# SBUF slots moved to multiples of 512 B, and a router with stationary weights in four column groups, in a two-block fp32 network on one core

## What is computed

```
def ec_moe(x, w_router, w_gate, w_up, w_down):
    B, N, _ = x.shape
    cap = CAPACITY_FACTOR * N // N_EXPERTS
    aff = jax.nn.softmax(jnp.einsum('bnd,de->bne', x, w_router).astype(jnp.float32), axis=-1)
    gates, idx = lax.top_k(jnp.swapaxes(aff, 1, 2), cap)
    bidx = jnp.arange(B)[:, None, None]
    xin = x[bidx, idx]
    h = jax.nn.silu(jnp.einsum('becd,edf->becf', xin, w_gate)) * jnp.einsum('becd,edf->becf', xin, w_up)
    out = jnp.einsum('becf,efd->becd', h, w_down) * gates[..., None].astype(x.dtype)
    return jnp.zeros_like(x).at[bidx, idx].add(out.astype(x.dtype))
```

## Time and profile before

| | us |
|---|---|
| median of 3 runs | 1737.58 (1735.65 to 1738.44) |
| the profiled execution's own time | 1737.63 |
| its span, first to last instruction | 1735.3 |
| TensorE busy | 1392.9 (80%) |
| VectorE busy | 593.1 (34%) |
| ScalarE busy | 431.6 (25%) |
| router of stage 0, and of stage 1 | from about 137, and from about 742 |
| units of stage 0 and of stage 1 reach their end | about 585, and about 1186 |

### The profile page before, as it was taken

One profiled execution on the slowest core, in us unless ns is written; L12 is line 12 of the kernel. 1 busy time (PEld: TensorE's weight loads), 2 busy tenths in 40 slices (PEclk: granted clock), 3 DMA queues, 4 the chain that ended last, 5 costly groups with the idle time before them and its releaser, 6 DMA issues.

```text
span 1735.3 us, 21553 instructions
## 1 busy us (share of the span) xinstructions
PE 1392.9 (80%) x9012; PEld 912.1 (53%) x9012; DVE 593.1 (34%) x993; ACT 431.6 (25%) x702; POOL 42.1 (2%) x53
## 2 busy tenths in 40 slices
PE   8999565574655999995765656559999999999997
PEld 8786121121211675751211212117999989889996
DVE  5663000010000366530000000004555566865556
ACT  4552000000000333420000000002444355653343
POOL 2000000000010012000000000000000000000000
PEclk9999888787888999998877878879999999999999
DMA  9858999999999943589999999999465764245650
GB/s 339 240 239 352 423 422 423 423 424 423 422 404 425 384 176 121 243 361 423 423 422 423 423 424 422 422 424 338 150 201 174 248 200 139 74 139 177 193 193 24
DMA packets 151333, 533.69 MB, mean 308 GB/s; under 512 B 10220, under 2 KB 73980, under 8 KB 105052
## 3 DMA queue, kind: packets, MB, share of 16 engines
q1 hardware_dynamic: 147392, 527.01, 77.6%
q10 hardware_dynamic: 2236, 2.25, 0.8%
q0 software_dynamic: 1632, 3.38, 0.6%
HBM read 529.98 MB, written 2.62 MB: 307 GB/s over the span
## 4 chain that ended last, share of the span: by engine, by line
PE 51%; DMA 37%; SPq 5%; DVE 4%; ACT 2%; issue 1%; POOL 0%; DVEq 0%; ACTq 0%; POOLq 0%
PE bank L1852 15%; DMA ring<-in_moe_w_up 14%; PE bank L703 12%; PE bank L1868 7%; DMA arena<-in_moe_w_down 4%; PE bank L1243 4%; DMA arena<-in_moe_w_up 4%; DMA moe_slots<-in_moe_w_up 3%; DMA xT<-in_moe_w_down 3%; DMA ring<-in_moe_w_down 3%; DMA gk_w<-in_moe_w_down 3%; PE bank L1283 3%; PE bank L541 3%; SPq L1430 2%; DMA moe_slots<-in_moe_w_down 1%; PE bank L322 1%
## 5 line engine op out<-in xcount | busy, mean ns | idle before, releaser
L622 DVE TENSOR_TENSOR w_lo<-ring,w_hi 128x1024 fp32r<-128x1024 f32 x187 | 228.6, 1224 | 191.6 <-ACT w_hi L617 191.1
L617 ACT ACTIVATE w_hi<-ring 128x1024 fp32r<-128x1024 f32 x187 | 197.9, 1060 | 266.2 <-PE bank L1852 150.2
L1243 PE MATMUL bank<-ring,arena 128*32 128x512 f32 x944 | 163.1, 706 | 82.9 <-DMA ring<-in_moe_w_up 52.8
L1852 PE MATMUL bank<-xT_hi,w_hi 128*128 128x256 f32 x704 | 199.8, 284 | 0.5 <-DVE xT_lo L504 0.3
L1852 PE MATMUL bank<-xT_hi,w_lo 128*128 128x256 f32 x704 | 199.2, 283 | 0.0
L1852 PE MATMUL bank<-xT_lo,w_hi 128*128 128x256 f32 x704 | 199.2, 283 | 0.0
L1283 PE MATMUL bank<-ring,arena 128*32 128x512 f32 x496 | 123.0, 809 | 82.7 <-DMA gk_w<-in_moe_w_down 27.8
L1401 DVE TENSOR_TENSOR arena<-arena,bank 64x512 f32<-64x512 f32 x32 | 22.1, 691 | 425.1 <-ACT arena L1341 425.1
L1852 PEld LDWEIGHTS bank<-xT_hi,w_hi 128*128 128x128 f32 x704 | 135.1, 192 | 1.5 <-issue 0.8
L1243 PEld LDWEIGHTS bank<-ring,arena 128*32 128x32 f32 x944 | 36.2, 121 | 189.3 <-issue 180.7
L1852 PEld LDWEIGHTS bank<-xT_lo,w_hi 128*128 128x128 f32 x704 | 135.1, 192 | 0.7
(11 more groups left out here) (302 smaller groups left out, 2365.4 us busy)
## 6 DMA issues: line engine op xcount, KB each, us to landing
ring<-in_moe_w_gate SPq DMA_DIRECT2D x70, 1024.0 KB, 25.8
ring<-in_moe_w_down SPq DMA_DIRECT2D x56, 1024.0 KB, 26.5
ring<-in_moe_w_up SPq DMA_DIRECT2D x48, 1024.0 KB, 26.6
arena<-in_moe_w_up SPq DMA_DIRECT2D x38, 1024.0 KB, 24.8
arena<-in_moe_w_gate SPq DMA_DIRECT2D x26, 1024.0 KB, 24.5
arena<-in_moe_w_down SPq DMA_DIRECT2D x26, 1024.0 KB, 25.8
moe_slots<-in_moe_w_up SPq DMA_DIRECT2D x22, 1024.0 KB, 26.9
moe_slots<-in_moe_w_down SPq DMA_DIRECT2D x22, 1024.0 KB, 27.1
```

Source lines behind the costliest of these rows:

```text
L617: nc.scalar.activation(dst, raw, ACT.Copy).then_inc(hi_ready, 1)
L622: nc.vector.tensor_tensor(lo, raw, hi.bitcast(F32), ALU.subtract).then_inc(split_ready, 1)
L1243: last = nc.tensor.matmul(ps[B_GU[j % 2]][32 * c:32 * c + 32, :], xin[:, j, k, :], w, start=(k == 0), stop=(k == KD - 1), tile_position=(0 ...
L1852: last = nc.tensor.matmul(ps[2 * s + f][:, n * SEQ:(n + 1) * SEQ], w_parts[wp][:, buf, k * P:(k + 1) * P], (xT_hi3, xT_lo3)[xp][:, k, :], ...
```

## The change

Three parts.

**Where tensors lie.** A tensor `align` of 384 B that nobody uses goes ahead of `ring`, and the tensors that hold slots follow one another: ring, xT, y, the split copies and moe_slots, h_slot, arena, gk_w, cst, then all small ones. As built, all 22 slots (the half in cst too) then start at a multiple of 512 B. No load and no order of loads changes.

**Router.** The weights (32 columns, 16 of the router and 16 that follow and are not used) are stationary, and x moves, 256 columns; part k goes to column group k mod 4 of bank 6. VectorE copies the four partial sums (128 x 256) to SBUF, and TensorE adds the groups by a matmul with `lg_sum`, four stacked identities of 16, which also brings the tokens to the partitions. The residual matmuls are spread in another way.

**Ranking and first choice from PSUM.** The first max and match_replace read the transposed affinities in PSUM, and the copy goes. The first group's picks read the ranks in PSUM, and the copy of the ranks follows. The ranks and two parts of the gathered x change banks for it.

```diff
+        sb("align", ALIGN_COLS)
         ring = sb("ring", 10 * SLOT)
+        xT, y = sb("xT", KD * SEQ), sb("y", NT * D)
...
+        moe_slots = sb("moe_slots", 4 * SLOT)
...
+        h_slot = sb("h_slot", SLOT)
+        arena_w = 13312
+        arena = sb("arena", arena_w)
+        gk_w = sb("gk_w", 2 * QK)
         cst = sb("cst", C_W)
...
-        rout_w = sb("rout_w", 2 * KD * NE)
-        gk_w = sb("gk_w", 2 * QK)
+        rout_w = sb("rout_w", 2 * KD * NE + NE)
+        lg_sum = sb("lg_sum", NE)
...
+        lg_part = arena[:, 0:SEQ]
...
-        B_GU, B_GA, B_HT, B_PT, B_DN, B_LG, B_AT, B_RK = (0, 1), (2, 3), 2, 3, (2, 3), 7, 1, 0
+        B_GU, B_GA, B_HT, B_PT, B_DN, B_LG, B_LP, B_AT, B_RK = (0, 1), (2, 3), 2, 3, (2, 3), 7, 6, 1, 1
+        rank_in = ps[B_RK][:, 64:64 + NT * NE].rearrange("p (i e) -> p i e", i=NT)
...
-            return ps[(2, 3, 1, 2)[k // 2]][:, k // 6 * 2 * P + k % 2 * P:k // 6 * 2 * P + (k % 2 + 1) * P]
+            return ps[(2, 3, 2, 1)[k // 2]][:, k % 2 * P:(k % 2 + 1) * P]
...
-                for i in range(NT):
-                    last = nc.tensor.matmul(ps[B_LG][:, i * NE:(i + 1) * NE], xT3[:, k, i * P:(i + 1) * P],
-                                            rout_w[:, (m * KD + k) * NE:(m * KD + k + 1) * NE],
-                                            start=(k == i == 0), stop=(k == KD - 1 and i == NT - 1))
+                q = k % 4
+                last = nc.tensor.matmul(ps[B_LP][32 * q:32 * q + 32, 0:SEQ], rout_w[:, (m * KD + k) * NE:(m * KD + k) * NE + 32],
+                                        xT3[:, k, :], start=(k < 4), stop=(k >= 4), tile_position=(0, 32 * q))
             last.then_inc(lg_psum, 1)
-            residual(pe, 0, range(4))
+            residual(pe, 0, range(2))
+            pe.wait_ge(lmax_ready, 2 * m + 1)
+            for i in range(NT):
+                last = nc.tensor.matmul(ps[B_LG][:, i * NE:(i + 1) * NE], lg_part[:, i * P:(i + 1) * P], lg_sum[:, :],
+                                        start=True, stop=True)
+            last.then_inc(lg_psum, 1)
+            residual(pe, 0, range(2, 6))
             pe.wait_ge(aff_ready, m + 1)
...
-            residual(pe, 0, range(4, KD))
+            residual(pe, 0, range(6, KD))
...
-            dve.wait_ge(lg_psum, m + 1)
+            dve.wait_ge(lg_psum, 2 * m + 1)
+            nc.vector.tensor_copy(lg_part, ps[B_LP][:, 0:SEQ]).then_inc(lmax_ready, 1)
+            dve.wait_ge(lg_psum, 2 * m + 2)
...
-            link(nc.vector.tensor_copy(affT[0], ps[B_AT][0:NE, 0:SEQ]))
             for r in range(CAP // 8):
-                c, src, dst = slice(8 * r, 8 * r + 8), affT[r % 2], affT[1 - r % 2]
+                c, src, dst = slice(8 * r, 8 * r + 8), affT[r % 2] if r else ps[B_AT][0:NE, 0:SEQ], affT[1 - r % 2]
...
-            link(nc.vector.tensor_copy(rank, ps[B_RK][:, 64:64 + NT * NE].rearrange("p (i e) -> p i e", i=NT)))
...
-                nc.vector.tensor_tensor(pick4, per_slot(rank, g), iota4, ALU.is_equal).then_inc(pick_ready, 1)
+                nc.vector.tensor_tensor(pick4, per_slot(rank if g else rank_in, g), iota4, ALU.is_equal).then_inc(pick_ready, 1)
+                if g == 0:
+                    link(nc.vector.tensor_copy(rank, rank_in))
...
+            nc.vector.memset(rout_w[:, 2 * KD * NE:], 0.0)
...
+            dve.wait_ge(ident_in, 16)
+            for q in range(4):
+                part = ident[:, 32 * q:32 * q + NE]
+                if q == 0:
+                    ins = nc.vector.tensor_copy(lg_sum[:, :], part)
+                else:
+                    dve.wait_ge(const_ready, 2 + q)
+                    ins = nc.vector.tensor_tensor(lg_sum[:, :], lg_sum[:, :], part, ALU.add)
+                ins.then_inc(const_ready, 1)
```

More of the change, by code:

```diff
@@ L100, in shape_constants @@
     return c, np.ascontiguousarray(band)
+ALIGN_COLS = 96
 class Unit:
@@ L179, in sem @@
             return ctx.enter_context(nc.semaphore(name))
+        sb("align", ALIGN_COLS)
         ring = sb("ring", 10 * SLOT)
-        cst = sb("cst", C_W)
-        lvl_mask = sb("lvl_mask", 7 * P, U8)
-        ln_rows, ln_cols = sb("ln_rows", P), sb("ln_cols", P)
-        mix_rows, mix_cols = sb("mix_rows", P), sb("mix_cols", 33)
-        pair_rows, pair_gb = sb("pair_rows", 2 * P), sb("pair_gb", 32)
-        xT, y = sb("xT", KD * SEQ), sb("y", NT * D)
-        gate_w = sb("gate_w", KD * 16)
-        glr_w = sb("glr_w", KD * 32)
-        rout_w = sb("rout_w", 2 * KD * NE)
-        gk_w = sb("gk_w", 2 * QK)
-        gate_b = sb("gate_b", 4)
-        lam_p = sb("lam_p", 4 * HD)
-        rel_t = sb("rel_t", A_HEADS)
-        ones = sb("ones", SEQ)
+        xT, y = sb("xT", KD * SEQ), sb("y", NT * D)
         with nc.sbuf_tensor("xT_hi", [P, KD * SEQ], F32R) as xT_hi, nc.sbuf_tensor("xT_lo", [P, KD * SEQ], F32R) as xT_lo, \
@@ L205, in program @@
         h_slot = sb("h_slot", SLOT)
+        arena_w = 13312
+        arena = sb("arena", arena_w)
+        gk_w = sb("gk_w", 2 * QK)
+        cst = sb("cst", C_W)
+        lvl_mask = sb("lvl_mask", 7 * P, U8)
+        ln_rows, ln_cols = sb("ln_rows", P), sb("ln_cols", P)
+        mix_rows, mix_cols = sb("mix_rows", P), sb("mix_cols", 33)
+        pair_rows, pair_gb = sb("pair_rows", 2 * P), sb("pair_gb", 32)
+        gate_w = sb("gate_w", KD * 16)
+        glr_w = sb("glr_w", KD * 32)
+        rout_w = sb("rout_w", 2 * KD * NE + NE)
+        lg_sum = sb("lg_sum", NE)
+        gate_b = sb("gate_b", 4)
+        lam_p = sb("lam_p", 4 * HD)
+        rel_t = sb("rel_t", A_HEADS)
+        ones = sb("ones", SEQ)
         stats = sb("stats", 64)
@@ L209, in program @@
         small = sb("small", 128)
-        arena_w = 13312
-        arena = sb("arena", arena_w)
         class Arena:
@@ L1320, in moe_scalar @@
         def moe_scalar(act, m):
-            act.wait_ge(lmax_ready, m + 1)
+            act.wait_ge(lmax_ready, 2 * m + 2)
             for i in range(NT):
```

## The result

| | before | changed |
|---|---|---|
| median, us | 1738.41 (1735.65 to 1738.6, 6 runs) | 1727.33 (1723.08 to 1731.92, 6 runs) |
| profiled execution, us (span) | 1737.63 (1735.3) | 1723.08 (1721.1) |

The ratio is 0.9938, interval [0.9924, 0.9953]. The change makes the kernel 11.1 us faster by the medians, where 18.9 were forecast; the median lies 1.3 us above the range that was given, 1713 to 1726. The profiled execution is the quickest of the six, so its 14.5 us of gain are more than the median's, and where the difference between executions comes from was a question of its own.

The account below looks back on a forecast made before the run. The prediction took the weight stream to bound the MoE stages, with a gap during the router. Alignment 16.1, router 2.6 and w_in 0.2 sum to 18.9 us off 1737.63: 1718.7 us, range 1713 to 1726.

Parts of the forecast that it names:

- Alignment: MoE weight streams: 134 units a stage newly in aligned slots gain 0.06 us each, 16.1 us in both stages.
- Rival A: MoE streams: the quick rate can't be had throughout; chance 0.10 in part, 0.07 in full.
- half is left: Rival A's case in which half the alignment gain in the MoE streams remains: 1726.7 us.
- Router: Both MoE stages, transposed x to stream restart: new matmuls and ranking from PSUM gain 2.6 us, bounds 0 and 4.4.
- The maximum at 139.7 to 140.1: Stage 0's router: with the new matmuls the maximum starts at 139.7 to 140.1 instead of 141.25 us.
- 0.2 for the first pick: Router's end: the first pick reads ranks from PSUM ahead of their copy, gaining 0.2 us a stage.
- TensorE's queue between the affinity transposes and the rank transposes decides: Router's ranking: TensorE's residual passes, not VectorE's chain, set the rank transposes' start; 0.6 and 0.55 us gained.
- The upper bound for this very case: Router in both stages: VectorE's chain decides, at the full clock; 1.55 + 0.41 + 0.2, twice, given as 4.4 us.
- w_in: Behind a MoE stage: ScalarE's wait for the first w_in unit shortens by 0.1 to 0.4 us, taken as 0.2.
- Rival B: MoE slots are quick by place, not alignment, and the change moves them: slower, 1739.3 to 1741.9 us; chance 0.03.
- C: Rival: TensorE's freed slots bound the MoE stream at changes of group; taken with Rival A, no chance of its own.

Follow-up runs that it names:

- e3: Weight stream alone, no computing: six phases of 62 units, slots 0, 128, 256, 160, 64 B past a multiple of 512 B, then mixed; 949.57 us.
- e1: The kernel before with the new places of the tensors alone, router and ranking as before; 1733.15 us, ratio 0.998.
- e4: The changed kernel unchanged, measured again on another occasion; 1731.87 us, ratio 0.9956.
- e9: The changed kernel with identity matmuls filling TensorE's waits ahead of the rank transposes and the GLA mixer's last level; 1724.48 us, ratio 0.9921.
- e10: The changed kernel unchanged, beside e9 on the same chip; 1728.15 us, ratio 0.9949.
- e8: Weight stream alone, seven phases of 50 units: one unit repeated, source off, both off, rows of 4 KB and 2 KB aligned and off; 928.67 us.
- e7: The changed kernel with every slot 128 B past a multiple of 512 B; 1740.63 us, ratio 1.0007.

## Why the prediction was wrong

- **Alignment, 16.1 us forecast, 8.4 measured (4.41 + 4.01). This is the step that failed:** "2.43 us for a unit in the aligned slots, 2.49 in the others, 0.06 each", times 134. The readings were right. But 2.43 was the pace of units that come behind slower ones and catch up; e3 shows it in its mixed phase and 2.453 where all are aligned. The units that were quick lost some 0.02, the others gained 0.032. The size is the same in all profiles: in the five with aligned slots (changed, e1, e4, e9, e10) the two streams take 425.7 to 426.8 and 423.7 to 423.9 us, in the four with the old places 430.0 to 430.3 and 427.5 to 427.8. Rival A named this, with "half is left" at 1726.7, and was given 0.10; that the median, 1727.33, lies so near is in part chance, since the router gave more than forecast and the clock took some back. What made me set it aside, that 4.85 and 4.86 stood behind one another and came back each turn, is just what catching up looks like as well.
- As a check of the size by the runs: a turn of 22 units takes 54.43 us in e3's mixed phase and 54.44 to 54.47 in the undisturbed turns of before, and 53.9 to 54.0 in e3's aligned phase and in the changed kernel. 7.5 turns of 0.46 are 3.5 us a stage, and the eight halves at the end give 0.42 and 0.26. The 0.5 and 0.3 us that are left are no more than one late unit costs, and not settled.
- The Trainium skill, "DMA: Bandwidth & Descriptors", section "How a descriptor splits into AXI transactions", has rows off a multiple of 256 B cost more, from which the prediction worked out 0.04 us a unit as an estimate. e3 measured 0.032, and 256 B is enough there, as the page has it. The page speaks of the side that is read; in e8 an unaligned source cost nothing, and the slot's side did. The other section cited, "Where 436 GB/s comes from", lets HBM bind a load at about 358 GB/s; this stream, with one core at work, sustained 427.
- **Router, 2.6 us forecast, 4.3 measured in the first profile.** The maximum at 139.7 to 140.1 was right (140.10), and so was 0.2 for the first pick (4.90 us from the rank transposes to the restart, 5.13 before). Right for the kernel before, and wrong for the changed one, was "TensorE's queue between the affinity transposes and the rank transposes decides": the queue got not 1.2 but 1.7 us shorter (20 residual passes in 2.40 us at the full clock, where 24 took 4.12), and then VectorE's chain decides and TensorE waits 0.98 us. So the copy counted, and from the maximum to the rank transposes the gain was 1.02 and 0.94 us instead of 0.1 and 0.55. In stage 0 these 1.02 are the copy (0.44), the affinity transposes sooner behind the maximum now that no half clock lies there (0.39), and what TensorE's queue had added before (0.19). The upper bound for this very case is given as 4.4, though its terms sum to 4.32. That the measured value is 4.32 too is chance: stage 0 gained 1.40 and stage 1 0.50 up to the maximum, not 1.55 each, and the ranking more. Where the half clock falls into the gathers, 1.5 us of it a stage go again.
- **w_in, 0.2 us forecast.** The first use comes 3.03 us behind the last landing before and 2.74 after: 0.3.
- **Not in the forecast:** the half clock behind TensorE's gaps. In the three profiles of the changed kernel it accounts for most of the differences, and its executions spread over 1723 to 1733 us. The forecast was made against one profiled execution of before with three such stretches, and I took the clock as given but for the router's. That the first profile of the changed kernel has none gives it most of the 1.94 us in GLA, which no edit made: e10, with 3.4 us of half clock there, has 155.82 us against its 154.10.
- Rival B (place, not alignment) is excluded by e3 and e7; C by TensorE's waits for each pair. e7, in which no slot is aligned, came at 1740.63, inside B's 1739.3 to 1741.9, but by alignment and not by place.

## What to carry to other kernels

A quicker pace that shows only for a few transfers in a row is not a pace for all: see first whether slower ones stand ahead of them, and measure the stream alone with all of them changed. Before a saving is worked out from the engine that ends a step, look how far behind the second one is, and redo it with every engine's saving at the clock that the changed step will have; here TensorE ended 0.2 to 0.3 us later than VectorE before, and 0.98 us earlier after. And a wait of TensorE that costs nothing by itself can cost 1.5 to 3.3 us by the clock granted behind it; filling two such waits with matmuls of the identity took 3.7 us off the median here.

## What the runs showed of the hardware

- The stream of 1 MB units in rows of 8 KB, into aligned slots, runs at a steady 2.453 us a unit, 427 GB/s, whether the source moves, repeats or starts 128 B off (e3, e8); rows of 4 KB give 420 GB/s and of 2 KB 408.
- Units behind a slow or late one come at 2.43 us for a while (e3's mixed phase, the changed kernel behind 408.67).
- A written row that starts 64, 128 or 160 B off costs 0.032 us a unit of 128 rows of 8 KB, twice that at 4 KB, about four times at 2 KB. 256 B off costs nothing.
- TensorE's half clock outside the streams came in stretches of 3.4 or 6.8 us, in some executions of one program and not in others: behind the wait of 3.67 us in eight of nine profiles, behind that of 0.98 in four of ten routers, and also at 58.9 us and in the old router with no wait ahead of it.
